# One hybrid decoder layer: output projection and router worked into the last head pair of the attention, convolution norm moved to head pair one

## The reference

```python
u = rms_norm(h, g_mix_pre)
proj = u @ w_in                                  # q | k | v of 12 heads x 64, then 2 x 256 conv channels
attn = dilated_attention(rotary(q), rotary(k), v)
conv = conformer_conv(c)                         # glu, depthwise conv of 31 taps, layer_norm, silu
mix = concatenate([attn, conv]) @ w_out
h = h + rms_norm(mix, g_mix_post)
u = rms_norm(h, g_ffn_pre)
ffn = moe_ffn(u)                                 # logits = u @ w_router, top 4 of 32 experts, clamped SwiGLU
h = h + rms_norm(ffn, g_ffn_post)
h = h + rms_norm((p @ w_ple) * sigmoid(h @ w_ple_gate), g_ple_post)
```

## Time and profile before

| | us |
|---|---|
| median of 3 runs | 2650.9 (2647.6 to 2654.27) |
| the profiled execution | 2655.26 |
| its span, first to last instruction | 2653.3 |
| TensorE busy | 2386.5 |
| VectorE busy | 1884.2 |
| ScalarE busy | 1452.9 |
| POOL busy | 242.4 |

### The profile page before, as it was taken

The page is one execution under the profiler, slowest core; times in us unless marked ns, Lnnn a source line. Parts: engine busy times, 40 slices in busy tenths (PEclk is TensorE's granted clock), DMA queues, the critical chain, the costliest instruction groups (busy, mean ns, idle before and its releaser), DMA issues.

```text
span 2653.3 us, 40578 instructions
## 1 busy us (share of the span) xinstructions
PE 2386.5 (90%) x10843; PEld 1603.3 (60%) x10844; DVE 1884.2 (71%) x2573; ACT 1452.9 (55%) x1604; POOL 242.4 (9%) x229
## 2 busy tenths in 40 slices
PE   6999999868846999999999999999999999994787
PEld 3455555434434777677777776777666767763343
DVE  4574555633346899889999998899777888983454
ACT  2113344432215777768777876777565767761233
POOL 1200001001221000100000010001010100001220
PEclk8999999888868999999999999999999999997899
DMA  6008800323205999989999998999797999994441
GB/s 184 20 12 283 272 21 23 114 84 72 71 32 189 309 358 364 337 286 366 363 353 366 370 348 298 332 360 362 265 312 237 319 309 318 363 318 151 149 148 52
DMA packets 446339, 629.40 MB, mean 237 GB/s; under 512 B 21209, under 2 KB 380633, under 8 KB 445894
## 3 DMA queue, kind: packets, MB, share of 16 engines
q1 hardware_dynamic: 391186, 532.20, 59.4%
q10 hardware_dynamic: 40304, 55.05, 5.8%
q0 software_dynamic: 14800, 41.51, 5.0%
HBM read 558.55 MB, written 68.57 MB: 236 GB/s over the span
## 4 chain that ended last, share of the span: by engine, by line
PE 69%; issue 10%; DVE 9%; DMA 5%; ACT 4%; DVEq 1%; SPq 1%; ACTq 1%; POOL 0%; POOLq 0%
PE bank L581 11%; PE bank L583 11%; PE bank L582 11%; PE bank L1267 6%; PE bank L1411 5%; PE bank L723 4%; PE bank L1290 3%; DMA raw<-in_w_down_dram 3%; DVE wlo L790 2%; PE bank L1257 2%; PE bank L630 2%; PE bank L1307 2%; PE bank L575 1%; PE bank L1336 1%; PE bank L553 1%
## 5 line engine op out<-in xcount | busy, mean ns | idle before, releaser
L1594 ACT ACTIVATE whi<-raw 128x2048 fp32r<-128x2048 f32 x456 | 871.4, 1916 | 382.6 <-PE bank L583 296.1
L790 DVE TENSOR_TENSOR wlo<-raw,whi 128x2048 fp32r<-128x2048 f32 x456 | 1036.3, 2284 | 50.2 <-PE bank L583 40.2
L581 PE MATMUL bank<-whi,xhi 128*128 128x512 f32 x1216 | 479.6, 394 | 0.0
L583 PE MATMUL bank<-wlo,xhi 128*128 128x512 f32 x1216 | 475.8, 391 | 0.0
L582 PE MATMUL bank<-whi,xlo 128*128 128x512 f32 x1216 | 475.7, 391 | 0.0
L581 PEld LDWEIGHTS bank<-whi,xhi 128*128 128x128 f32 x1216 | 229.5, 189 | 63.9 <-issue 19.7
L583 PEld LDWEIGHTS bank<-wlo,xhi 128*128 128x128 f32 x1216 | 229.1, 188 | 49.2
L582 PEld LDWEIGHTS bank<-whi,xlo 128*128 128x128 f32 x1216 | 229.2, 188 | 48.2
L581 PE MATMUL bank<-whi,hhi 128*128 128x512 f32 x608 | 243.2, 400 | 0.0
L582 PE MATMUL bank<-whi,hlo 128*128 128x512 f32 x608 | 237.8, 391 | 0.0
L583 PE MATMUL bank<-wlo,hhi 128*128 128x512 f32 x608 | 237.4, 390 | 0.0
(11 more groups left out here) (288 smaller groups left out, 3116.2 us busy)
## 6 DMA issues: line engine op xcount, KB each, us to landing
raw<-in_w_gate_up_dram SPq DMA_DIRECT2D x608, 512.0 KB, 5.5
raw<-in_w_down_dram SPq DMA_DIRECT2D x152, 1024.0 KB, 8.7
expert_rows<-zeros ACTq DMA_DIRECT2D x1, 33280.0 KB, 105.0
expert_rows<-ysb ACTq DMA_DIRECT2D x38, 512.0 KB, 7.0
xall<-in_x_dram SPq DMA_DIRECT2D x8, 512.0 KB, 12.2
uT<-in_w_out_dram SPq DMA_DIRECT2D x1, 4096.0 KB, 13.2
xr<-in_x_dram SPq DMA_DIRECT2D x8, 512.0 KB, 6.9
h_scratch<-h SPq DMA_DIRECT2D x8, 512.0 KB, 2.9
```

The lines of the kernel that those rows point to most:

```text
L581: pe.matmul(dst, stat_hi[:, kt], hi, start=False, stop=False)
L583: return pe.matmul(dst, stat_hi[:, kt], lo, start=False, stop=last)
L790: dve.tensor_tensor(wlo[:, c % LO], raw[:, c % RAW], whi[:, c % HI].bitcast(F32), ALU.subtract).then_inc(lo_ready, 1)
L1594: act.activation(whi[:, c % HI], raw[:, c % RAW], ACT.Copy).then_inc(hi_ready, 1)
```

## The change

What it does:

- `stage2_end` and the barrier are gone. The buffers of stage 3 no longer have memory of their own behind the attention: they lie in buffers of the attention that are dead by then (h1 in qT and kT of the even pairs, u2 in qraw and rotc, x tiles in wq and wk, gains in glu, small tables in conv and qsw, u2T and scratch in the rotary tables), so SyncE loads them while pair 5 runs, behind w_out.
- In pair 5 the output projection is TensorE's filler: 14 of a tile's 16 matmuls in the tile's own step (`out_part`), the two that need pair 5's own output one step later (`out_last`). Scores of pair 5 use banks 0 and 1 alone, so the second chunk of scores waits for the mask of the first; the projection uses banks 2 and 3.
- ScalarE first copies the projection to h1 (`rows_in`); norms follow one step behind, the u2 transposes, logits and choice two steps behind, ranks and list positions three steps behind (`turn_u2`, `logits`, `choose`, `ranks`, `place`). The u2 transposes go in two halves through bank 7, which logits and ranks use too. The copy of mix tiles is gone.
- The convolution norm lies in pair 1, steps 8 to 14, both halves at once in banks 2 and 3.
- The loops of stage 3 are written out.

The core of the diff (the mapping of buffers and the bodies that only changed names are left out):

```diff
+        early, later = Carve(conv[:, 1]), Carve(qsw[:])
...
-        MEAN = {4 * NT + 6: 0, 4 * NT + 7: 1}
-        VAR = {5 * NT + 1: 0, 5 * NT + 2: 1}
-        SQUARES, ROOT, AFFINE, GATES, CONV_OUT = 5 * NT, 5 * NT + 3, 5 * NT + 4, 5 * NT + 5, 5 * NT + 6
+        LN = NT
+        MEAN, SQUARES, VAR, ROOT, AFFINE, GATES, CONV_OUT = range(LN, LN + 7)
...
+        def score_bank(s, c, h):
+
+            return banks(h) if s > LASTP else banks(2 * c + h)
...
             sp.dma_start(wout, w_out[0].rearrange("(k p) n -> p k n", p=P)).then_inc(wout_in, 16)
+            for s in range(2):
+                sp.dma_start(xr[s], x[0, s * P:s * P + P, :]).then_inc(xr_in[s], 16)
+            sp.wait_ge(ln_dve, 13)
+            sp.dma_start(gpost, g_mix_post[0].partition_broadcast(P)).then_inc(vec3_in, 16)
...
-            sp.wait_ge(stage2_end, 4)
...
+                elif not last:
+                    pe.wait_ge(u2t_ready, 2 * t + 1)
+                dst = banks(4 + half) if last else banks(7)
...
+                if s == LN + 3:
+                    pe.wait_ge(ln_dve, 6)
...
+            for i in range(NT):
+                s = LASTP + i
+                if i < NT - 1:
+                    scores(s + 1, 0)
+                if i > 0:
+                    out_last(i - 1)
+                for h in range(2):
+                    turn_probs(s, 0, h)
+                ranks(i - 3)
+                turn_u2(i - 2, 0)
+                out_part(i, 0, OUT_K[0])
+                if i < NT - 1:
+                    scores(s + 1, 1)
+                if part(i) == 2:
+                    for h in range(2):
+                        turn_probs(s, 1, h)
+                out_part(i, 0, OUT_K[1])
+                turn_u2(i - 2, 1)
+                out_part(i, 1, OUT_K[0])
+                values(s)
+                out_part(i, 1, OUT_K[1])
+                logits(i - 2)
+            out_last(NT - 1)
+            ranks(NT - 3)
+            for half in range(2):
+                turn_u2(NT - 2, half)
+            logits(NT - 2)
+            ranks(NT - 2)
...
+            for i in range(NT):
+                s = LASTP + i
+                mix(s - 1)
+                if i > 0:
+                    rows_in(i - 1)
+                probs(s)
+                if i > 0:
+                    root_mix(i - 1)
+                if i > 1:
+                    columns_u2(i - 2, 0)
+                if i > 0:
+                    square_h(i - 1)
+                    root_h(i - 1)
+                if i < NT - 1:
+                    exp(s + 1)
+                if i > 1:
+                    columns_u2(i - 2, 1)
...
+            for i in range(NT):
+                s = LASTP + i
+                if i < NT - 1:
+                    mask(s + 1, 0)
+                if i > 2:
+                    place(i - 3)
+                if i > 0:
+                    mix_var(i - 1)
+                    mix_norm(i - 1)
+                if i < NT - 1:
+                    mask(s + 1, 1)
+                    row_max(s + 1)
+                if i > 0:
+                    h_var(i - 1)
+                if part(i) == 2:
+                    probs(s)
+                if i > 0:
+                    h_norm(i - 1)
+                if i < NT - 1:
+                    normalise(s + 1)
+                if i > 1:
+                    choose(i - 2)
```

More of the change, by code:

```diff
@@ L421, in hold @@
             eng.sem_inc(tick, 1)
-        D3 = 30
+        A3 = 5
+        N3 = 7
+        R3 = 23
+        M_AT, RANK_AT = 10, 14
+        LASTP = (PAIRS - 1) * NT
+        OUT_K = ((0, 1, 2, 3), tuple(k for k in range(4, KD) if k != PAIRS - 1))
         F5 = 8
@@ new lines, in logits, with ranks @@
+            def logits(t):
+                if t < 0:
+                    return
+                if t == 0:
+                    pe.wait_ge(vec3_in, 64)
+                pe.wait_ge(u2t_ready, 2 * t + 2)
+                for k in range(KD):
+                    mm = pe.matmul(logit_bank(t), u2T[:, k], wr[:, k], start=(k == 0), stop=(k == KD - 1))
+                mm.then_inc(logit_done, 1)
+            def ranks(t):
+                if t < 0:
+                    return
+                pe.wait_ge(pick3, R3 * t + M_AT)
+                pe.matmul(banks(7)[:, 0:E], tri, M, start=True, stop=False)
+                pe.matmul(banks(7)[:, 0:E], ones[:], Macc, start=False, stop=True).then_inc(rank_done, 1)
@@ L1440, in _ @@
+            out_last(NT - 1)
+            ranks(NT - 3)
+            for half in range(2):
+                turn_u2(NT - 2, half)
+            logits(NT - 2)
+            ranks(NT - 2)
+            for half in range(2):
+                turn_u2(NT - 1, half)
+            logits(NT - 1)
+            ranks(NT - 1)
+            pe.wait_ge(pick3, R3 * NT)
             pe.matmul(banks(0)[:, 0:E], ones[:], Macc[:], start=True, stop=True).then_inc(cnt_done, 1)
@@ L1523, in _ @@
                           zeros[:].unsqueeze(1).to_broadcast([P, reps, 256])).then_inc(rows_zero, 16)
[L1524 removed]
+            for s in range(LASTP):
                 if s > 0:
@@ L1821, in mask_max @@
                                           ALU.max, ALU.mult).then_inc(negmax, 1)
+            def mask_max(s):
+                for c in range(2):
+                    mask(s, c)
+                row_max(s)
             def probs(s):
@@ L1841, in _ @@
             normalise(0)
-            for s in range(STEPS):
+            for s in range(LASTP):
                 i, g = s % NT, s // NT
```

572 lines of the change are left out of this document (281 added, 291 removed).

## The result

| | before | changed |
|---|---|---|
| median of runs on one chip | 2652.6 (4 runs, 2647.6 to 2655.1) | 2579.5 (4 runs, 2578.6 to 2585.0) |
| ratio, with its 95% interval | 1 | 0.9731 [0.971, 0.9751] |
| profiled execution, span | 2653.3 | 2577.8 |

What follows compares the result with a forecast made beforehand. TensorE, busy 90% of the span, bounds the kernel, so only its idle or slow time returns. Terms -79.4, -3.1 and +17 sum to -65.5 us: 2585.5 us against the median of 2650.9, range 2568 to 2614.

Steps and rivals of the forecast that it cites:

- last pair's first scores to counting matmul: Stretch from the last pair's scores to the matmul counting tokens per expert: 200.6 us against 280.0, -79.4 us.
- The last pair as TensorE work: Last pair: attention 29.6, projection 108.0, router 23.6 and changes of kind of work 3, together 164 us.
- Waits left in it: TensorE waits left in the last pair: 4 x 1 us, 0.7 in steps 1 to 3, 3 in step 0; 9 us.
- The tail: From the end of the last logits inside the pair to the counting matmul: 27.6 us.
- work costed at nothing: Early loads, last pair's table loads, POOL's list writes, weight pieces: all expected to fit in spare time, 0 us.
- The end of pair 4: Conv-mean matmuls and their VectorE passes leave pair 4's end, and P-tile copies start earlier: -3.1 us.
- The norm in pair 1: Convolution norm in pair 1, where TensorE has no idle time to give: +17 us, bounds 11.5 and 30.
- Table loads: ScalarE table switches priced at the trace's 1.28 us each, not the Trainium skill's 2.66 us.
- The clock: Rival: clock falls inside the last pair's steps, 2.7 us in seven steps, 19 us, giving 2604; chance 0.14.
- The longer chain of the step: Rival: the last pair's step chain exceeds TensorE's work, six steps grow 4 us, 24 us, giving 2610; chance 0.13.
- the router's round trip: Rival: TensorE waits it out in six last-pair steps, 18.8 us each, 113 us, giving 2698; chance 0.03.
- w_out was in time: Projection weights issued more than 25 us before the last pair; rival of late arrival 5 us, 2590; chance 0.02.

Runs made afterwards that it cites:

- e4: Changed kernel with the first half of the u2 transposes behind the step's first four projection matmuls; 2574.6 us, 0.9704 of the kernel before.
- e11: Changed kernel with the convolution norm spread over pairs 1 to 4 and the first u2 transposes behind the first projection matmuls; 2568.5 us, 0.9693 of the kernel before.
- e9: Changed kernel with ten more 128x512 matmuls, feeding no result, in the tail's waits; 2576.5 us, 0.9711 of the kernel before.
- e5: Changed kernel with two more ScalarE table loads in each of the last pair's seven steps; 2579.1 us, 0.9719 of the kernel before.
- e6: Changed kernel without interleaving: the last pair's attention first, then projection, norms and router, still no barrier; 2596.8 us, 0.9793 of the kernel before.
- e8: Kernel before with only the convolution norm moved to pair 1; 2648.5 us, 0.9985 of the kernel before.
- e1: Changed kernel with the convolution norm one head pair later, in pair 2; 2576.8 us, 0.9722 of the kernel before.
- e3: Changed kernel with the convolution norm one step earlier, from step 7; 2575.7 us, 0.971 of the kernel before.
- e7: Changed kernel without the convolution's layer norm and gating; median not comparable, counting matmul starts at 690.6 us.
- e10: Changed kernel with the convolution norm spread over pairs 1 to 4, at most one piece per step; 2569.9 us, 0.9696 of the kernel before.
- e13: Changed kernel with spread norm, later u2 transposes and both halves of the scaling in the middle of pair 3; 2565.1 us, 0.9666 of the kernel before.
- e12: Changed kernel with spread norm, later u2 transposes and the scaling's second half moved to pair 3's fifth step; 2568.5 us, 0.9691 of the kernel before.

## Why the prediction was right, point by point

| term | forecast | measured | difference |
|---|---|---|---|
| last pair's first scores to counting matmul | -79.4 | -89.0 | -9.6 |
| end of pair 4 | -3.1 | -2.4 | +0.7 |
| convolution norm in pair 1 | +17 | +19.0 | +2.0 |
| ahead of the first scores | 0 | -1.9 | -1.9 |
| behind the counting matmul | 0 | -1.3 | -1.3 |
| sum | -65.5 | -75.5 | -10.0 |

- **The last pair as TensorE work, 164 us.** The eight windows from 515 to 680 us hold 158.7 us of busy time. The projection was sized rightly (22 records at 515 to 528 take 9.45 us, 0.86 for two, as assumed); logits add 1.71 us to the chain behind running matmuls, and not the 1.99 that they took behind a wait in the old loop, at clock 1.00 in both, and the 3 us for changes of kind of work are not there. 5 us too much.
- **Waits left in it, 9 us.** 164.4 us from first scores to last logits less 158.7 is 5.7, so 3 too much. The repeated wait was the right one, five times 0.74 to 1.03 us for four times 1 us, and e4 and e11 remove it.
- **The tail, 27.6 us.** 26.7, with the logits of 3.6 us as forecast. The chain of the working was the right one. e9 shows a second limit right behind it, the landing of POOL's list writes, which the prediction had under work costed at nothing by the 23 us of a step; in the tail the placing of two tiles is only some 10 us apart. In the changed kernel it cost nothing yet.
- **The end of pair 4.** -3.1 us in eleven of the thirteen kernels of the study; the changed kernel and e5 lost 0.7 of it to clock (0.66 from 510 to 515 us in both).
- **The norm in pair 1, +17 us.** The size was right within 1 us where the clock fell once (16.1 and 16.5 in e6 and e8; 16.6 and 16.4 at other places in e1 and e3) and 2 to 3.5 us too small where it fell twice, which the sum had only as a rival for the last pair. The place was right too: TensorE's largest wait stands ahead of step 12's scores, released by the variance pass. The mechanism was right only in part, and that the parts add up to 17 is luck. Its largest term, 7.8 us, had the reciprocal hold up a mask, with TensorE's variance matmuls hidden in that wait. In the trace the reciprocal costs no wait; the matmuls (3.70 us) stand in the open, and 4.82 us for the two banks come on top, 8.5 us. The two waits of pair 1 without the norm (1.76 and 1.23 us at this place in e7) are gone in return, and the lower clock behind the wait takes 2.2 us of that back. The root shows nothing where 1.5 us were given, a wait of 1.86 us stands behind the scaling (1 given), and one of 1.74 us behind the last product, which was to be hidden.
- **Table loads.** The row's 1.28 us was the right price: e5 doubles the switches and the time is the same, where by the Trainium skill ("ScalarE: Activation LUTs", "What ACT_TABLE_LOAD costs") its 14 extra ones would be some 37 us of ScalarE, an estimate by 2.66 us each. What its advice costs when it is broken depends on slack: nothing here but in step 2.
- **The rivals.** The clock did not fall in the steps of the last pair of the changed kernel. In e4 and e9 it did in step 0 (0.89 and 0.79), with waits of about 0.8 and 0.3 us ahead as in e10, e11 and e13, where it stayed at 1.00; in e5 it fell in step 2. The longer chain of the step fell too: what VectorE and ScalarE do in a steady step is 12 and 10.5 us of 23. TensorE did not sit out the router's round trip (the 9.5 us in that rival's price stand in no row). w_out was in time, but only just, and the prediction's reading was wrong: from 484.93 to the last pair's first scores at 500.78 it is 16 us in the kernel before, and 13 in the changed one, not more than 25. SyncE issued w_out at 505.4 us, it took 13.0 us to land, and the first projection matmul started at 518.64. In nine other kernels that matmul waited 0.3 to 0.5 us for it (all but e5, e6 and e8).

Against the profiled executions the total was 10 us off, against the medians 6, since the profiled execution of before lay 4.4 above its median. That the other four terms cancel is luck: the two outside the change (-1.9 and -1.3) lie within what these stretches do by themselves, since the first scores of pair 0 start at 199.6 to 202.7 us over all kernels. Nearly all of the error is in one term, and for one reason: where I had no row for a small thing (a change of kind of work, a wait in steps 0 to 3), I rounded up.

## What to carry to other kernels

A stage that waits on its own chain is worth filling even when its work is only moved: in 43 us of bare attention TensorE was busy for 34, and weaving was worth 21 us. But over half of the last stretch's gain (48 of 89 us) came from loads that no longer wait for a barrier and from norms and router placed one to three tiles behind. Auxiliary work that must go into a dense stage can cost little more than TensorE's own part if it is cut into pieces and put in the steps where its engine has slack: 9 us spread, of which 7.4 are TensorE's, against 16 to 20.5 in one run of steps. When a stretch is made shorter, look again at what was costed at nothing in it: w_out and the list writes both had plenty of time by the forecast; w_out landed 0.2 us ahead of its use, and the list writes were waited for 3.30 us in e9. Before moving a piece, read which instance of a line the wait stands behind: two instances of one line misled me once.

## What the runs showed that I had not expected

- **VectorE's normalise and POOL's multiply exclude each other.** Two passes over 896 columns take 1.28 us alone, and 3.38 us when POOL's multiply starts 0.33 us after the first, in e3 and e10 to e13 alike. The two records of e10 (ns: least, median, most) and a product of the norm beside POOL in e13:

```profile
L1925 DVE TENSOR_SCALAR S<-S,small x2: 686/1730/2774, 379.3 to 379.9; 128x896 f32<-128x896 f32 x2
```

```profile
465.39 3.37 DVE L1968 TENSOR_TENSOR xall<-conv,glu 128x1024 f32<-128x1024 f32 x1
```

  The first pass is as quick as ever, the second ends only at 382.7, behind POOL's end at 382.2; POOL's multiply takes 2.57 us for 2.35 alone. L1968 takes 1.22 us alone and started 0.12 us after POOL's multiply. Masks, which read PSUM, take their usual 0.69 us beside POOL (315.06 in the kernel before), and the reciprocal of 512 columns takes 3.34 us beside it (e10), half of the 6.55 for 1024. The Trainium skill, "SBUF — State Buffer", section "Who interferes with whom", calls this an exclusive lock on a shared port pair; the trace agrees. In the kernel before POOL starts 0.3 us behind the passes, by timing alone: what releases it is ScalarE's copy of the projection. In e10 to e13 the passes start 1.24 us later against POOL, and ahead of their exp stands the load back from the root of step 20 (e13):

```profile
376.17 1.28 ACT L1564 ACT_TABLE_LOAD   x1
```

- **A short stand of TensorE can cost twice.** 4.82 us of waiting in pair 1 are followed by matmuls at 3.04 us for 1.98. But it isn't certain: besides the place behind pair 1 above, after the same 1.9 us wait, the next six matmul records took 4.31 and 4.26 us in e10 and e11 (granted clock 0.66 from 388 to 393) and 2.84 in e12. What decides it is left open.
- **Extra matmuls raise the clock and hardly the speed** if something else bounds the stretch: in e9 the clock went from 0.59 to 0.95, and 1.8 of 26.7 us came back, as the list writes then held up the last tile.
